# Moving the expert output rows of a hybrid decoder block (top-4 of 32 experts) to their tokens by 32-row TensorE products on one Trainium2 core

## The reference, cut to what matters

```python
x = x + jnp.concatenate([o_a, o_b], axis=-1) @ w_out[l]
h2 = _rmsnorm(x, norm2_g[l]).reshape(B * S, D)
x = x + _moe(h2, router_w[l], router_b[l], w_up[l], b_up[l], w_down[l], b_down[l]).reshape(B, S, D)
return _rmsnorm(x, final_norm_g)

def _moe(h, router_w, router_b, w_up, b_up, w_down, b_down):
    logits = (h @ router_w + router_b).astype(jnp.float32)
    top_vals, top_idx = lax.top_k(logits, TOP_K)
    gates = jax.nn.softmax(top_vals, axis=-1)
    ...
    def expert_block(args):
        xb, e = args
        u = xb @ w_up[e] + b_up[e]
        return _clamped_swiglu(u) @ w_down[e] + b_down[e]
    ...
    y = ybuf[dest] * gates.reshape(-1)[order][:, None].astype(ybuf.dtype)
    return jnp.zeros((N, D), h.dtype).at[sorted_tok].add(y)
```

## Time and profile before

| | us |
|---|---|
| median of 3 runs | 1322.87 (1322.38 to 1324.13) |
| the profiled execution | 1323.94, mean granted clock 0.988 |
| its span in the profile | 1322.0 |
| TensorE matmul records (PE) busy | 1216.3 (92%) |
| VectorE / ScalarE / GpSimd busy | 536.8 (41%) / 305.6 (23%) / 185.5 (14%) |
| DRAM read / written | 441.46 MB / 13.63 MB |

### The profile page before, as it was taken

How to read it: one execution, slowest core, us unless ns; L and a number is a source line. 1 busy time by engine, 2 the same in 40 slices (tenths; PEclk the granted TensorE clock), 3 DMA queues, 4 the chain that set the end, 5 groups by cost and what they waited for, 6 DMA issues and landing times.

```text
span 1322.0 us, 30062 instructions
## 1 busy us (share of the span) xinstructions
PE 1216.3 (92%) x12799; PEld 594.8 (45%) x12800; DVE 536.8 (41%) x1134; ACT 305.6 (23%) x614; POOL 185.5 (14%) x199
## 2 busy tenths in 40 slices
PE   6999999999999999999989999898989898989973
PEld 5888876675343434343333333333333333433332
DVE  5667645566334523423232323232332323242315
ACT  6365424321011211211112111111111111111113
POOL 0000001100022122121212021121212121212012
PEclk9999999998999999999999999999999999999997
DMA  9523229038899999999999999999999999999993
GB/s 292 161 65 95 65 69 379 1 117 344 352 400 418 422 413 416 422 414 426 413 423 416 424 414 424 414 422 419 416 422 413 426 416 424 417 425 415 427 376 125
DMA packets 70974, 454.12 MB, mean 344 GB/s; under 512 B 7657, under 2 KB 36813, under 8 KB 46160
## 3 DMA queue, kind: packets, MB, share of 16 engines
q1 hardware_dynamic: 64832, 438.59, 80.7%
q0 software_dynamic: 6000, 13.49, 3.7%
HBM read 441.46 MB, written 13.63 MB: 344 GB/s over the span
## 4 chain that ended last, share of the span: by engine, by line
PE 53%; DMA 39%; DVE 3%; ACT 1%; issue 1%; POOL 1%; POOLq 0%; SPq 0%; DVEq 0%
DMA w_raw_pair<-w_up 22%; PE psum L1951 20%; PE psum L1971 13%; DMA w_raw_pair<-w_down 12%; PE psum L1704 5%; PE psum L1701 3%; DMA w_in_raw<-w_in 2%; PE psum L1790 2%; PE psum L1989 2%; DMA expert_sums<-expert_rows 1%; PE psum L1838 1%; PE psum L1814 1%; PE psum L1777 1%; PE psum L1855 1%; DMA expert_rows<-y_rows,scatter_rows 1%
## 5 line engine op out<-in xcount | busy, mean ns | idle before, releaser
L1951 PE MATMUL psum<-w_raw_pair,x_slots_turned 128*32 128x512 f32 x4928 | 553.1, 595 | 46.4 <-DMA w_raw_pair<-w_up 46.2
L1951 PEld LDWEIGHTS psum<-w_raw_pair,x_slots_turned 128*32 128x32 f32 x4928 | 152.4, 110 | 399.6 <-issue 329.7
L1971 PE MATMUL psum<-w_raw_pair,a_slots 128*32 128x256 f32 x4992 | 278.2, 379 | 12.8 <-DMA w_raw_pair<-w_down 12.7
L1971 PEld LDWEIGHTS psum<-w_raw_pair,a_slots 128*32 128x32 f32 x4992 | 157.6, 110 | 123.6 <-DMA w_raw_pair<-w_down 22.6
L1492 DVE STREAM_TRANSPOSE x_slots_turned<-gathered_quarters 128x256 f32<-128x256 f32 x74 | 43.4, 632 | 276.6 <-PE psum L1951 276.6
L853 ACT ACTIVATE lin<-psum 128x768 f32<-128x768 f32 (+1 forms) x32 | 22.6, 705 | 547.0 <-PE psum L1951 547.0
L1530 DVE TENSOR_TENSOR x_rows<-x_rows,psum 128x512 f32<-128x512 f32 x120 | 77.0, 684 | 124.5 <-PE psum L1989 124.3
L1497 DVE STREAM_TRANSPOSE a_slots<-glu 128x768 f32<-128x768 f32 (+1 forms) x31 | 26.3, 849 | 190.0 <-PE psum L1971 190.0
L647 POOL COPY gather_quarters<-row_quarters 128x2 int32 (+1 forms) x30 | 15.0, 500 | 555.8 <-DVE x_slots_turned L1492 507.4
L666 POOL DMA_INDIRECT expert_rows<-y_rows,scatter_rows x48 | 65.1, 1357 | 181.1 <-DVE y_rows L1549 171.3
L863 ACT ACTIVATE y_parts<-psum,gate_t 32x256 fp32r<-32x256 f32 x128 | 59.8, 467 | 111.8 <-PE psum L1971 109.8
(11 more groups left out here) (295 smaller groups left out, 1060.2 us busy)
## 6 DMA issues: line engine op xcount, KB each, us to landing
w_raw_pair<-w_up SPq DMA_DIRECT2D x128, 2048.0 KB, 41.1
w_raw_pair<-w_down SPq DMA_DIRECT2D x64, 2048.0 KB, 40.6
w_in_raw<-w_in SPq DMA_DIRECT2D x28, 512.0 KB, 3.8
w_buf<-w_out SPq DMA_DIRECT2D x4, 1024.0 KB, 9.1
expert_rows<-zero_rows SPq DMA_DIRECT2D x5, 512.0 KB, 7.0
x_rows<-x SPq DMA_DIRECT2D x4, 512.0 KB, 5.1
x_rows<-x SPq DMA_DIRECT2D x1, 2048.0 KB, 17.1
normed_rows<-h_rows SPq DMA_DIRECT2D x4, 512.0 KB, 2.6
```

The lines of the kernel that those rows point to most:

```text
L1951: ins = pe.matmul(U[quarter(j), g, :], slots, up_columns(w, j), start=False, stop=(c == UPC - 1))
L1971: ins = pe.matmul(banks[quarter(j), g, :], slots[:, g, 2 * c + h, :], raw[q.slot(m)][:, at_w:at_w + 256], start=False, stop=(c == DNC - 1 ...
```

## The change

Nothing is scattered any more and expert_rows is gone, with its zero rows at the start (5 transfers of 512 KB), its 48 indirect DMAs, the reading back (4 transfers of 512 KB) and GpSimd's four additions. All 32 experts go the same way:

- ScalarE writes the gated, rounded rows of a group in one instruction of 128x256, VectorE the remainder in one of 128x256: partitions 32j to 32j+31 keep the column quarter j where PSUM has it.
- The selection matrix of a group (128x512) has the group's 32 slots four times below each other (slot_tokens, made once by `token_rows`). `token_sels` writes one per group.
- TensorE multiplies by quarters (`move_turn`, L1895 in the changed kernel): stationary is 32x128 of the selection, moving 32x256 of y_part, quarter j of the rows into PSUM bank 4+j. Per expert 4 token tiles x n groups x 2 parts x 4 quarters = 32n products, in two turns of two token tiles each: 96 for BIG, 64 for LESS, 2560 in all. Two tiles share the four banks 4 to 7, one in each half.
- A turn stands behind up chunk 2 and one behind up chunk 5, in every step from 2 on.
- VectorE adds a tile (128x1024, out of four banks) in one instruction, 4 per expert.
- The down products of group 2 lie in bank 4, so the down bias of a BIG expert waits for all four additions; that of a LESS expert only for y_low.
- The last down products go to bank 0, and expert 30's two turns stand among expert 31's down chunks.

Cut to its core:

```diff
+            def token_rows(src, dump, cols):
+                for g in range(BIG):
+                    for j in range(4):
+                        dve.tensor_scalar(slot_tok[quarter(j), g, cols], src[quarter(g), :], dump[quarter(g), :], None, ALU.add)
...
-            def scatter(q):
-                rows = row_q[0:STEP, :, bass.ds(expert_at(q.expert), 1)].rearrange("p g o -> p (g o)")
-                pool.tensor_copy(IDXT[0:STEP, :], rows).then_inc(S("scatter_quarters"), 1)
...
-                pool.wait_ge(y_ready, q.nth * 2 + 2)
...
-                for g in range(BIG):
-                    pool.indirect_dma_start(acc_dram, bass.IndirectOffsetOnAxis(IDXS[0:STEP, g:g + 1], 0), Y[quarter(g), :], None,
-                                            compute_op=ALU.add, bounds_check=SEQ - 1, oob_is_err=False).then_inc(acc_added, 16)
-                pool.wait_ge(acc_added, (q.nth + 1) * BIG * 16)
...
-            sp.wait_ge(acc_added, BIGS * BIG * 16)
-            sp.wait_ge(chunk_used, step_chunks(NE - 1).count(0))
-            for i in range(TT):
-                sp.dma_start(XF[:, i, :], accv[:, i, :]).then_inc(S(f"xf_in{i}"), 16)
...
+            def y_highs(n, column, banks):
+                for g in range(n):
+                    ins = act.activation(YP[0][g][:, :], banks[:, g, :], ACT.Copy, scale=gate_t[:, g, bass.ds(column, 1)])
+                    if g:
+                        ins.then_inc(y_high, 1)
+            def outputs(q, down_chunks_end):
                 act.wait_ge(chunk_used, down_chunks_end)
+                if q.nth:
+                    act.wait_ge(moved, q.nth * 2)
+                y_highs(q.n, expert_at(q.expert), Yp2)
...
+            def y_lows(highs, n, column, banks):
+                for g in range(n):
+                    if g != 1:
+                        dve.wait_ge(y_high, highs + max(g, 1))
+                    ins = dve.scalar_tensor_tensor(YP[1][g][:, :], banks[:, g, :], gate_t[:, g, bass.ds(column, 1)],
+                                                   YP[0][g][:, :].bitcast(F32), ALU.mult, ALU.subtract)
+                ins.then_inc(y_low, 1)
+            def token_sels(n, column, sels):
+                for g in range(n):
+                    ins = dve.tensor_scalar(sels[g][:, :], tokens[:, :], slot_tok[:, g, bass.ds(column, 1)], None, ALU.is_equal)
+                ins.then_inc(token_sel, 1)
+            def add_tile(i, first_bank):
+                x_tile, half = X[:, i, :].rearrange("p (j f) -> p j f", j=4), slice(i % 2 * 256, i % 2 * 256 + 256)
+                dve.tensor_tensor(x_tile, x_tile, PS[:, first_bank:first_bank + 4, half], ALU.add).then_inc(added, 1)
+            def add_moved(k, tiles):
+                for i in tiles:
+                    if i % 2 == 0:
+                        dve.wait_ge(moved, k * 2 + (i // 2 + 1))
+                    add_tile(i, MOVE_BANK)
...
+            def move_turn(turn, n, sels, bank, first=True, last=True):
+                for i in (2 * turn, 2 * turn + 1):
+                    for g in range(n):
+                        for part in range(2):
+                            for j in range(4):
+                                ins = pe.matmul(PS[:, bank + j, i % 2 * 256:i % 2 * 256 + 256], sels[g][quarter(j), i * P:(i + 1) * P],
+                                                YP[part][g][quarter(j), :], start=(first and i % 2 + g + part == 0),
+                                                stop=(last and g == n - 1 and part == 1), skip_group_check=True)
+                ins.then_inc(moved, 1)
+            def move(k, turn, n, adds):
+                if turn == 0:
+                    pe.wait_ge(token_sel, k + 1)
+                    pe.wait_ge(y_low, k + 1)
+                    if not isinstance(k, int) or k:
+                        pe.wait_ge(added, adds)
                 else:
+                    pe.wait_ge(added, adds + 2)
+                move_turn(turn, n, SELT, MOVE_BANK)
...
                 for c in range(UPC):
                     up_chunk(q, c, n, p > 1)
-                    if moved is not None and moved.n == LESS and 3 <= c < 7:
-                        move(moved.nth, moved.nth, LESS, 2 * c - 6, MOVE_BANKS)
-                        move(moved.nth, moved.nth, LESS, 2 * c - 5, MOVE_BANKS)
+                    if moved is not None and c in (2, 5):
+                        move(moved.nth, c // 3, moved.n, moved.nth * TT)
...
+                    pe.wait_ge(y_low, moved.nth + 1)
+                    if n_before == BIG:
+                        pe.wait_ge(added, moved.nth * TT + TT)
```

242 lines of the change are left out of this document (58 added, 184 removed).

## The result

| | before | after |
|---|---|---|
| median of the runs | 1322.73 us (1322.38 to 1324.13, 4 runs) | 1309.57 us (1307.95 to 1311.56, 4 runs) |
| ratio, 95% interval | | 0.9899 (0.9882 to 0.9916) |
| profiled execution, span | 1323.94, 1322.0 | 1309.24, 1307.4 |

The change makes the kernel 13 us faster. The forecast was 1295 us, 28 faster. The direction was right, the time lies in the range, and less than half of the forecast gain is there. The median moves by 13.2 us and the span of the profiled executions by 14.6.

A forecast was written before the change was run, and what follows sets the result against it. DMA was to stay the bound, closely followed by TensorE: last down product at 1273 us plus a tail of 21.2 gives a span of 1294.2 against 1322.0, hence 1295 us as median; range 1287 to 1314.

The forecast's parts named there:

- DMA, 16 x 1.6 = 25.8 us less: Expert part: dropping the three scatters of each of 16 BIG experts frees 1.6 us of DMA time apiece, 25.8 us.
- TensorE, a pair of 59.3 us: Expert part: a pair of steps on TensorE grows from 56.45 to 59.3 us through the moves by quarters.
- TensorE alone: End of the expert part if only TensorE limited it: last down product at 1269.5 us, median time 1291.6.
- the downs keep their length: Down products on TensorE: two groups' downs taken at 6.9 us from the earlier trace, with GpSimd's gathers costing nothing.
- DMA is still the bound, by 1.6 us a pair: Expert part: a pair of steps needs 60.9 us on DMA against 59.3 on TensorE, 1.6 us of slack instead of 6.1.
- rival C: Even steps' down bias waits for late VectorE additions: 1.7 us in each of 14, 24 us, about 1317; chance 0.04.
- The tail: From the last down product to the end: 21.2 us against 24.0 before, 2.8 us less.
- A: Moves on TensorE: quarters overlap only in part, 35 to 40 ns a product, 1307 to 1320 us; chance 0.13.
- B: Moves on TensorE: the quarters' loads queue, 119 ns a product, 230 us more, about 1522 us; chance 0.11.
- D: Expert part: the freed DMA share doesn't go to weights as DRAM is the limit, 1320 us; chance 0.05.
- 59 to 61: Sign in the profile: length in us of a pair of steps in the expert part.
- last down product at 1270 to 1276: Sign in the profile: when in us the expert part's last down product ends, with 21 us to the end.

The follow-up runs named there:

- e2_before_no_scatter: The kernel before without its 48 scatters (the large experts' rows are missing from the result): 1299.9 us, ratio 0.9839.
- e5_after_again: The changed kernel, unaltered, measured again: 1301.09 us, ratio 0.9842 to the kernel before.
- e9_four_rows: The changed kernel with each gather from the fifth expert on fetching 4 rows instead of 128 (rows missing from the result): 1294.04 us, ratio 0.9782.
- e3_moves_twice: The changed kernel with every turn's products issued twice, but for two turns at the end (2496 more products): 1367.68 us, measured once.

## Why the prediction was wrong

**DMA, 16 x 1.6 = 25.8 us less: mis-sized, 20.1.** The window with three scatters and the one without gave 0.69 MB a set. Over 600 us it is 247.50 - 242.75 = 4.75 MB more weights, with 600 / 62.56 = 9.6 large experts, so 0.50 MB or 1.2 us each; the landing of the last expert's first down pair gives 20.1 / 16 = 1.26. But e2_before_no_scatter, which leaves out nothing but the scatters, gives 21.9 us, 1.4 a set, and 248.27 - 242.75 = 5.52 MB over the same 600 us, 1.4 us each as well. (Its pair lands 25.7 us earlier than before, but its expert part also began 2.6 us earlier.) So one window of 15 us against one other was too small a sample, and the sum had no term for what the changed kernel itself takes from DMA: from 300 to 1200 us it brings 365.95 MB of weights (e5_after_again) where e2_before_no_scatter brings 367.60, some 4 us less. A start 1.8 us later and 1.59 MB of instructions for 1.33 are parts of that; the rest is open. The 5.7 us that the DMA term is short lift the forecast of 1295 to 1301, which is what the kernel takes in the two jobs without the stall that timed it (1301.1 and 1301.2).

**TensorE, a pair of 59.3 us: right where there is no stall (59.36), 60.4 to 60.5 in the measured result.** The terms held: 30 ns for 29 a product, step 3's biases at 403.98 in e5_after_again, whose expert part began 0.85 us earlier than in the trace before, so 404.83 for 404.8, two turns within an up part +3.54 us for a pair of large ones (3.5) and 2.58 for small ones (2.6). What the sum lacked is the stall. From one down bias to the next it costs 1.0 us in each odd step and 0.1 in each even one: the eleven pairs from 455.29 to 1120.21 us take 664.92 us, 60.45 each. The first three steps lose 2.8 us more. Up to the down bias of step 30 the kernel after takes 1240.49 - 364.71 = 875.78 us from that of step 1, and e9_four_rows 1226.11 - 366.68 = 859.43: 16.4 us of stall. "TensorE alone" ends at 1272.3 in e9_four_rows, which began 2.0 us later, so 1272.3 - 2.0 + 16.4 = 1286.7 with the stall, and the trace of the kernel after has 1286.68. It replaces the DMA end of 1277.75, so the stall costs 8.9 us of the end, which is what lies between 1309.6 and 1301.1 (8.5).

**The miss of 14.6 us is thus 8.5 of stall and some 6 of DMA.** The step that failed first is that the downs keep their length: the prediction took them from the earlier trace rows and, of GpSimd, said "It keeps the gathers; its waits were never on the path". Its waits aren't. Its issuing is, under a condition that stays open. The second is the DMA term: 1.6 us a set where 1.4 is measured, and nothing for what the change itself costs DMA.

**DMA is still the bound, by 1.6 us a pair: half right.** The weights' need of 60.9 us a pair was well read (25.17 MB at 247.5 MB in 600 us is 61.0). But TensorE begins with weights in hand and runs at its own 59.36 until about 1100 us before it meets the transfers (e5_after_again: its waits for weights are 1.6 us up to 1200 us and 4.3 behind), so DMA shows only at the end. The two-sums reckoning, the later of both ends, was the right form.

**VectorE, rival C: refuted.** The addition takes 1218 ns and no down bias waits. The cover was worked out wrongly: 3.4 - 0.1 - 2.44 is 0.9 us and not 0.7, and twice the addition would have cost 1.6 us a step and not 1.7. In the trace the second addition ends at 756.53 and the down bias starts at 757.52, so the cover is 1.0. **The tail**: 20.7 us for 21.2.

**Rivals.** A and B fell with 30.0 ns in e3_moves_twice, D with e2_before_no_scatter. The measured time lies in the stretch that I gave to rival A (1307 to 1320) and looks like it. It is not it: TensorE is the bound as A says, but by its downs, not by its moves. That the time lies in the range is luck of this kind: the range reached to 1314 for A's sake. A forecast of a number can be met by the wrong mechanism.

**The signs.** 2560 products of 30 ns, full DMA, weights' waits under 20 (none), the indirect queue at 2.2%, no wait at the even down bias, 21 us of tail: all as said. Pairs at 60.4 were inside "59 to 61", too wide a sign to show the stall. Only "last down product at 1270 to 1276" failed.

## What to carry to other kernels

When a change makes another engine the bound, list what else runs beside that engine's densest stretch, since it was free only while there was slack; here the cure is one wait that moves GpSimd's three gathers behind the next up chunk. It gave 1299.5 to 1301.2 us in the three jobs that had it, one of them with the stall's condition. A gain from removed transfers is better read from a run of the old kernel that only leaves them out (here 1.4 us a set) than from two short windows of the trace (1.6). And where the result doesn't fit, run the very same kernel again before explaining it: four edits (late gathers, doubled products, half the products, a shifted program) seemed to cure the stall, and three of them only stood in a job that had none.

## What the hardware showed unexpectedly

- Two or three indirect DMA instructions of GpSimd (1.0 us each, 1.3 apart) beside TensorE's 32-column products of 256 columns make TensorE stand still for some 0.8 us in all of 7, without a semaphore. It is there with 4 rows a gather too, and longer (1.6 us), and absent beside GpSimd's copies and with one gather. In the even steps, with two gathers beside 192 products, it is 0.1 to 0.3 us (0.5 to 0.6 in step 2), and 0.9 to 1.1 in step 1, with three gathers beside 192.
- It comes in 4 of the 8 jobs that could tell, alike for all loadings in a job, and one chip number had it once and not the other time. What the condition is stays open, as does what GpSimd and TensorE share there. Where the instruction fetches fall doesn't make it. In each of the 13 odd steps from 430 to 1156 us of the kernel after, one packet of the instruction queue falls into the first 11 us behind the down bias. It comes anywhere from the second of them to the tenth, while the stall is 0.7 to 0.8 us in all but the first step (1.4). The same fetches stand beside 7.09 us in e5_after_again.
- Four 32-row fp32r products of 256 columns, one to a row quarter, take 120 ns together with their loads. The full-height product of 512 columns starts every 230 ns, 115 for 256 columns, so by this estimate four quarters side by side give 4 x 115 / 120 = 3.8 times one alone.
- Three scatters of 32 rows of 4 KB that add in DRAM take some 1.4 us of all DMA engines from the weights (e2_before_no_scatter), for 0.3 MB.
